# Trunk layer step on one core: the first channel products take turns with the modulation, and the last expert's rows are finished on chip

## The reference

```python
sh1, sc1, g1, sh2, sc2, g2 = jnp.split(mod, 6)         # mod = silu(c) @ w_mod + b_mod, w_mod is 1024 x 6144
u = rmsnorm(x, norm1_g) * (1 + sc1) + sh1
z = u @ w_in                                           # 1024 x 5120: xr, xv, xg, ga, gb
...                                                    # RG-LRU branch on xr, conformer branch on xv, xg
merged = sigmoid(ga) * (y_a @ w_rnn_out) + sigmoid(gb) * (y_b @ w_conv_out)
x = x + g1 * (merged @ w_out)
v = rmsnorm(x, norm2_g) * (1 + sc2) + sh2
x = x + g2 * ec_moe(v, w_router, w_e1, w_e3, w_e2)     # 16 experts, each takes its top 64 + 16 tokens
y = rmsnorm(x, final_norm_g)                           # for both token sets
```

## Time and profile before

| | |
|---|---|
| time, median of 3 runs | 1774.56 us (1773.85 to 1776.88) |
| the profiled execution | 1772.81 us, of it 1771.0 us span from first to last instruction |
| TensorE busy | 1655.0 us, 93% of the span |
| VectorE, ScalarE busy | 1401.4 us (79%), 1096.5 us (62%) |
| data moved | 492.49 MB, 278 GB/s over the span |

### The profile page before, as it was taken

How to read it: one execution, slowest core, us unless ns; L and a number is a source line. 1 busy time by engine, 2 the same in 40 slices (tenths; PEclk the granted TensorE clock), 3 DMA queues, 4 the chain that set the end, 5 groups by cost and what they waited for, 6 DMA issues and landing times.

```text
span 1771.0 us, 20907 instructions
## 1 busy us (share of the span) xinstructions
PE 1655.0 (93%) x7922; PEld 1168.0 (66%) x7922; DVE 1401.4 (79%) x1306; ACT 1096.5 (62%) x839; POOL 262.5 (15%) x124
## 2 busy tenths in 40 slices
PE   4698889899999949999999999999999999999994
PEld 0298779688888736666666666666666666666662
DVE  0429999997335468998998898898988989989985
ACT  3325544552522347777778777777777777777773
POOL 2002536420000010102201101102101012022020
PEclk8699999999999969999999999999999999999997
DMA  9811120122325289999999999999999999999993
GB/s 392 321 53 48 53 71 30 60 72 71 98 72 167 100 328 397 361 383 389 374 377 386 372 380 384 370 381 384 374 389 370 379 392 363 384 389 363 382 336 126
DMA packets 142559, 492.49 MB, mean 278 GB/s; under 512 B 11258, under 2 KB 23706, under 8 KB 139457
## 3 DMA queue, kind: packets, MB, share of 16 engines
q1 hardware_dynamic: 137280, 475.75, 71.3%
q0 software_dynamic: 3776, 11.09, 2.8%
q10 hardware_dynamic: 1472, 5.25, 0.7%
HBM read 478.91 MB, written 13.16 MB: 278 GB/s over the span
## 4 chain that ended last, share of the span: by engine, by line
PE 82%; DVE 10%; DMA 5%; issue 1%; ACT 1%; another core or an unknown queue 0%; SPq 0%; DVEq 0%; POOLq 0%; ACTq 0%
PE ps L1803 60%; PE ps L1618 12%; DVE ring L1116 5%; DMA ring<-in_w_mod 3%; PE ps L1580 2%; PE ps L1678 2%; PE ps L1730 1%; DVE ring L1144 1%; PE ps L1783 1%; DVE a_lo L1050 1%; PE ps L1515 1%; PE ps L1595 1%; DVE ring L1091 1%; DMA xn_dram<-ring 1%; PE ps L1777 0%
## 5 line engine op out<-in xcount | busy, mean ns | idle before, releaser
L1420 DVE TENSOR_TENSOR ring_lo<-ring,w_hi 128x2048 fp32r<-128x2048 f32 x384 | 872.2, 2289 | 109.5 <-ACT w_hi L918 109.5
L918 ACT ACTIVATE w_hi<-ring 128x2048 fp32r<-128x2048 f32 x384 | 734.9, 1918 | 260.1 <-PE ps L1803 259.9
L1803 PE MATMUL ps<-w_hi,xe_hi 128*80 128x512 f32 x1024 | 403.1, 394 | 2.1 <-DVE xe_lo L1481 2.1
L1803 PE MATMUL ps<-ring_lo,xe_hi 128*80 128x512 f32 x1024 | 402.8, 393 | 0.0
L1803 PE MATMUL ps<-w_hi,xe_lo 128*80 128x512 f32 x1024 | 400.6, 391 | 0.0
L1803 PEld LDWEIGHTS ps<-w_hi,xe_hi 128*80 128x80 f32 x1024 | 151.8, 148 | 86.5 <-issue 2.9
L1803 PEld LDWEIGHTS ps<-w_hi,xe_lo 128*80 128x80 f32 x1024 | 151.8, 148 | 84.3 <-issue 0.7
L1803 PEld LDWEIGHTS ps<-ring_lo,xe_hi 128*80 128x80 f32 x1024 | 151.8, 148 | 80.9 <-issue 0.5
L653 POOL DMA_INDIRECT acc_dram<-ya,idx_s x16 | 75.5, 4717 | 864.7 <-remote 864.7
L1803 PE MATMUL ps<-w_hi,h_hi 128*80 128x512 f32 x512 | 203.1, 397 | 0.0
L1803 PE MATMUL ps<-ring_lo,h_hi 128*80 128x512 f32 x512 | 201.1, 393 | 0.0
(11 more groups left out here) (266 smaller groups left out, 2008.8 us busy)
## 6 DMA issues: line engine op xcount, KB each, us to landing
ring<-in_w_e SPq DMA_DIRECT2D x192, 2048.0 KB, 9.7
ring<-in_w_mod SPq DMA_DIRECT2D x24, 1024.0 KB, 15.8
ring<-in_w_in SPq DMA_DIRECT2D x12, 1024.0 KB, 5.1
ring<-in_w_in SPq DMA_DIRECT2D x16, 512.0 KB, 3.7
xr<-in_x_sample SPq DMA_DIRECT2D x8, 512.0 KB, 5.5
ring<-in_w_rnn_out SPq DMA_DIRECT2D x8, 512.0 KB, 3.8
ring<-in_w_conv_out SPq DMA_DIRECT2D x8, 512.0 KB, 3.9
ring<-in_w_out SPq DMA_DIRECT2D x8, 512.0 KB, 4.2
```

Source lines behind the costliest of these rows:

```text
L918: eng.activation(w_hi[m % 2][:, 2 * half:2 * half + 2, :], chunk(m)[:, 2 * half:2 * half + 2, :], ACT.Copy).then_inc(unit_hi, 1)
L1420: eng.tensor_tensor(w_lo(m)[:, 2 * half:2 * half + 2, :], w, w_hi[m % 2][:, 2 * half:2 * half + 2, :].bitcast(F32), ALU.subtract)\
L1803: ins = eng.matmul(ps[0:CAP, bank + b, :], x[:, k0 + kk, :], w[:, kk, 512 * b:512 * b + 512], start=first and kk == 0 and n == 0, stop=las ...
```

## The change

Five parts belong together at the start, three at the end.

Start: (1) SP puts two `w_in` tiles after the eighth `w_mod` piece and the third after the sixteenth. (2) The tokens are transposed and copied unscaled out of PSUM while the first third of mod is still being loaded; the copy of the column vectors (`cols`) comes behind it on DVE, the reciprocal of the norm before it. (3) Scale and shift are applied in place in SBUF, and the split runs by pairs of 128-row blocks (four pairs) instead of halves. (4) The first round of the channel loop is taken out of the loop and its six groups stand between the second and third thirds of mod on TensorE; the gates begin the loop, and the other banks of `MOD_BANKS` and `MOD_TURN_BANKS` keep the two apart. (5) ACT and DVE are reordered to suit.

End: (6) the last expert stands outside the loop and leaves out the unused rows. (7) When the fifteenth addition has landed and two of the ring's slots are free, SP reads `acc_dram` back, and the five tiles are normed and stored without the last expert. (8) POOL gathers the last expert's 80 rows of `acc_dram`; its `ye` is added to them on DVE, squared, normed, and written by two indirect transfers over the stored rows.

The core of the diff:

```diff
-MOD_BANKS = (4, 5, 4)
+MOD_BANKS = (4, 6, 2)
+MOD_TURN_BANKS = (7, 7, 3)
...
+        fin = ring[:, 0:NT * D].rearrange("p (t d) -> p t d", t=NT)
...
@@ sync @@
-            for n in range(2 * KD):
+            for n in range(KD):
                 load_mod(n)
-            for kind in range(3):
-                load_a(0, kind)
+            load_a(0, 0)
+            load_a(0, 1)
+            for n in range(KD, 2 * KD):
+                load_mod(n)
+            load_a(0, 2)
...
-            eng.wait_ge(scattered, 16 * E)
+            product_done(eng, E - 1, NSLOT)
+            product_done(eng, E - 1, NSLOT + 1)
+            eng.wait_ge(scattered, 16 * (E - 1))
             for t in range(NT):
-                eng.dma_start(xr[:, t, :], acc_dram[P * t:P * t + P, :]).then_inc(fin_loaded[t], 16)
+                eng.dma_start(fin[:, t, :], acc_dram[P * t:P * t + P, :]).then_inc(fin_loaded, 16)
...
@@ gpsimd, after the loop of E - 1 @@
+            eng.indirect_dma_start(out=xe, out_offset=None, in_=acc_dram,
+                                   in_offset=bass.IndirectOffsetOnAxis(ap=idx_t[:, E - 1:E], axis=0)).then_inc(xe_loaded, 16)
...
+            eng.wait_ge(out_stored, 16 * NT)
+            eng.wait_ge(out_ready, NT + 1)
+            for out, column, lo, hi in ((a["y_sample"][0], 0, 0, CAP_S), (a["y_prompt"][0], 1, CAP_S, CAP)):
+                eng.indirect_dma_start(out=out, out_offset=bass.IndirectOffsetOnAxis(ap=idx_out[0:hi - lo, column:column + 1], axis=0),
+                                       in_=ye[lo:hi, :], in_offset=None).then_inc(rows_patched, 16)
@@ scalar @@
+            for k in range(KD):
+                eng.wait_ge(xt_turned, k + 1)
+                eng.activation(uT[:, k, 0:NP], ps[:, 2 * (k % 2) + 1, 0:NP], ACT.Copy).then_inc(xt_prompt, 1)
             copy_mod(0)
...
+                for k in (2 * j, 2 * j + 1):
+                    eng.activation(uT[:, k, 0:NP], uT[:, k, 0:NP], ACT.Identity, scale=a1[:, k, 0:1], bias=modc[:, k, 0:1])\
+                        .then_inc(ut_prompt, 1)
...
+                eng.activation(u_hi[:, 2 * j:2 * j + 2, :], uT[:, 2 * j:2 * j + 2, :], ACT.Copy).then_inc(u_hi_ready, 1)
@@ vector @@
+                    eng.tensor_scalar(uT[:, k, NP:N], uT[:, k, NP:N], a1[:, k, 1:2], modc[:, k, 1:2], ALU.mult, ALU.add)\
+                        .then_inc(ut_sample, 1)
...
+            output(E - 1)
+            eng.wait_ge(ye_ready, E)
+            eng.wait_ge(xe_loaded, 16 * (E + 1))
+            eng.tensor_tensor(ye, ye, xe, ALU.add).then_inc(ye_ready, 1)
...
+            eng.scalar_tensor_tensor(out=ye, in0=ye, scalar=rstat[0:CAP, 3, 0:1], in1=gf[0:CAP, :],
+                                     op0=ALU.mult, op1=ALU.mult).then_inc(out_ready, 1)
@@ tensor @@
+            channel_products(0, 0, first=True)
+            channel_products(0, 1)
+            eng.wait_ge(cols_ready, 1)
+            for n in range(KD, 2 * KD):
+                mod_products(n)
+            channel_products(0, 2)
+            mod_turn(1)
+            eng.wait_ge(modc_ready, 2)
+            channel_products(0, 3)
+            eng.wait_ge(xr_copied, 2)
+            for n in range(2 * KD, 3 * KD):
+                mod_products(n)
+            channel_products(0, 4)
+            mod_turn(2)
+            eng.wait_ge(modc_ready, 3)
+            channel_products(0, 5)
+            with eng.Fori(0, 3) as i:
+                gate_products(i)
+                for n in range(6):
+                    channel_products(i + 1, n)
+            gate_products(3)
```

More of the change, by code:

```diff
@@ L401, in trunk_layer @@
         gf_loaded = sem("gf_loaded")
-        fin_loaded = [sem(f"fin_loaded{t}") for t in range(NT)]
+        fin_loaded = sem("fin_loaded")
+        last_prompt_idx = sem("last_prompt_idx")
+        rows_patched = sem("rows_patched")
         fin_ssq = sem("fin_ssq")
@@ L645, in _ @@
             step.restart()
-            with eng.Fori(0, E) as i:
+            with eng.Fori(0, E - 1) as i:
                 eng.wait_ge(xe_turned, i + 2)
@@ L797, in _ @@
             a_high(0, 0, first=True)
-            a_high(0, 1, first=True)
+            eng.wait_ge(a12_ready, 1)
+            u_prompt(0)
+            u_prompt(1)
+            u_high(0)
+            u_prompt(2)
+            u_high(1)
+            u_prompt(3)
+            u_high(2)
+            u_high(3)
+            a_high(0, 1, first=True)
+            eng.wait_ge(cols_ready, 1)
+            lam = cols[:, C_TAB + 8 * G_LAM:C_TAB + 8 * G_LAM + 16]
+            step.did(eng.activation(sp[:, 0, :], lam, ACT.Abs))
+            step.wait()
+            eng.activation(sp[:, 1, :], sp[:, 0, :], ACT.Exp, scale=-1.0).then_inc(exp_lam_ready, 1)
+            step.restart()
+            a_high(0, 2, first=True)
+            eng.wait_ge(consts_ready, 4)
+            copy_xr(0)
+            copy_mod(1)
             copy_mod(2)
-            a_high(0, 2, first=True)
-            copy_xr(0)
+            eng.wait_ge(mod_used, 3 * KD)
             first_tap(0)
@@ L1002, in _ @@
             inverse_root(ssq_ready, NT, ms_ready, root_ready, 0, NT)
+            eng.wait_ge(root_ready, 1)
+            eng.reciprocal(rstat[:, 3, :], rstat[:, 2, :]).then_inc(r_ready, 1)
+            for k in range(KD):
+                eng.wait_ge(xt_turned, k + 1)
+                eng.tensor_copy(uT[:, k, NP:N], ps[:, 2 * (k % 2), :]).then_inc(xt_sample, 1)
             eng.wait_ge(cols_turned, 1)
             eng.tensor_copy(cols[:, 0:C_TAB + 8 * G_NLAM], ps[:, 6, 0:C_TAB + 8 * G_NLAM]).then_inc(cols_ready, 1)
-            eng.wait_ge(root_ready, 1)
@@ L1006, in _ @@
[L1006 removed]
+            eng.wait_ge(cols_ready, 1)
             mod_columns(0)
             modulated(a1, 1, C_N1)
[L1009 to L1016 removed]
+            eng.wait_ge(xt_sample, KD)
@@ L1458, in dve_expert @@
                         split_h(i, 1)
-                        modulate_xe(i + 2)
-                split_xe(i + 2)
+                        if not final:
+                            modulate_xe(i + 2)
                 if not final:
+                    split_xe(i + 2)
                     for m in range(2):
                         split_piece(i + 1, m)
-                output(i)
-                step.restart()
+                    output(i)
+                    step.restart()
+            eng.tensor_scalar(idx_out[:, 0:1], idx_t[0:CAP_S, E - 1:E], float(NP), None, ALU.subtract).then_inc(idx_ready, 1)
             split_piece(0, 0)
@@ L1538, in turn_row_tile, with turn_x @@
                 ins.then_inc(done, 1)
+            def turn_x(k):
+                turn_row_tile(xn1, k, 4, xt_turned, (xt_sample, xt_prompt))
             eng.wait_ge(silu_ready, 1)
-            for n in range(KD):
+            for n in range(5):
                 mod_products(n)
+            eng.wait_ge(xn1_ready, NT)
+            turn_x(0)
+            turn_x(1)
+            turn_x(2)
+            mod_products(5)
+            turn_x(3)
+            turn_x(4)
+            turn_x(5)
+            mod_products(6)
+            turn_x(6)
+            turn_x(7)
             eng.wait_ge(vec_loaded, 16 * 13)
@@ L1792, in _, with expert @@
                     ins.then_inc(xe_turned, 1)
-            with eng.Fori(0, E) as i:
+            def expert(i, final):
                 eng.wait_ge(xeT_ready, i * 2 + 1)
@@ L1829, in _ @@
                 eng.wait_ge(h1_silu, i * 2 + 2)
-                turn_xe(i + 2)
+                if not final:
+                    turn_xe(i + 2)
                 hidden_product(9)
@@ L1834, in _ @@
                 hidden_product(11)
+            with eng.Fori(0, E - 1) as i:
+                expert(i, False)
+            expert(E - 1, True)
 _INS = ["x_prompt", "x_sample", "state_rglru", "c", "c_ctx", "norm1_g", "norm2_g", "w_mod", "b_mod", "w_in",
```

146 lines of the change are left out of this document (71 added, 75 removed).

## The result

The changed kernel takes 1741.51 us (median of four runs, 1740.48 to 1741.78), the kernel before beside it 1774.20: a ratio of 0.9814 [0.9802, 0.9827], 32.7 us less. The forecast was 1743.5, 2.0 us too high. The profiled execution has a span of 1740.0 us, against 1771.0.

What follows compares the result with a forecast made beforehand. Two places bound it: the first round's 288 products, on which DVE's chain hangs, and 24 us behind the last product. 21 + 9 = 30 us off 1772.81 gave 1742.8; 1743.5 was called, range 1735 to 1757.

Steps and rivals of the forecast that it cites:

- Start: First round's six groups: done earlier, so DVE's chain starts 21 us sooner, carried to the end; bounds 10 and 25.
- Step 1: Normed rows ready near 23 us, token transposes between pieces 4 and 7; first third's columns at 42 us, before and after.
- Step 2: DVE's token scaling and splits: last quarter ready at 53.9 us; first product near 46.7, group 1 at 56.5, group 2 at 63.5.
- Step 3: Loads: piece 15 waits for piece 8's buffer, SP's queue stops, piece 15 lands at 69.5 us; products 8 to 15 end at 70.8.
- Step 4: Groups 3 and 4, last third's pieces: group 4 ends at 86.2 us, piece 23 lands at 92.8, with 2 us of waiting.
- rival (d): TensorE, interrupted by waits, stays at half clock up to group 6: costs 58 us, total 1800 us; chance 3%.
- Step 5: Group 6 ends at 108.9 us, before 130.5; DVE's chain starts 21.6 us earlier, taken as 21 and carried to the end.
- rival (e): DVE's first round waits for gate weights or next tiles; only the end gains: 1764 us, 3%; no end gain: 1773, 2%.
- Experts: Expert loop: body unchanged; last expert drops eight transposes, 0.55 us; the small scatter-index operation on DVE costs nothing.
- End: Behind the last product: final norm mostly done earlier, last transfer lands at 1761.7 against a span end of 1771.0; 9 us gained.
- the bound "3 us sooner": Last two indirect transfers: landing 3 us sooner than estimated would make the end's gain 12 us.
- the sign of 7 to 8 us: Kernel's end: the span was to end 7 to 8 us behind DVE's last scaling.

Runs made afterwards that it cites:

- the earlier tile: The changed kernel with the third `w_in` tile loaded ahead of `w_mod` piece 15 instead of behind it: 1737.07 us, 4.4 us less than the changed kernel.

## Why the prediction was right, point by point

**Start** (forecast 21 us, measured 22.7 at the split that opens DVE's stretch). The order of events is as forecast. That the number fits is in part luck, since two errors cancel in it.
- Step 1 is the worst: the columns of the first third stood at 37.0 and not at 42. I had kept TensorE's work "the same in another order" behind rows that end at 39.1; but the rows now start at 17.62, the transposes fall between pieces that were late anyway, and from 22 to 36 us the clock was full. That made 5 us.
- Step 2: the first product came at 41.78, 4.9 us ahead of 46.7, but at the lower clock to about 47. Groups 1 and 2 are done at 58.73 against the 63.5 forecast. At full clock a group took 7.2 to 7.3 us and not 7.0.
- Step 3 came true: the loads stood still from 54 to 60 us (DMA share 0.04 and less), and this cost TensorE nothing at piece 15, since products 8 to 15 ran in one go (7.08 us from 58.73).
- Step 4 names 2 us of waiting for piece 23, but its own sum holds only 0.2 (86.2 + 7 x 0.91 = 92.6, landing at 92.8). Measured were 2.35: TensorE came 5.1 us sooner (81.13 against 86.2), and the piece only 3.0 (89.8). The lower clock behind the wait (about 1.5 us) was rival (d) on a small scale, a few us and not 58. Three of the kernels above kept full clock behind waits of 2.20, 2.25 and 2.38 us, so the wait alone does not decide it. Group 6 ended at 107.8 against 108.9: of 5 us won by step 1 about 4 were lost again here, and the earlier tile shows that the wait can be had back.
- Step 5: DVE's chain hung on the sixth group and ACT's rounding, and the gain was carried on (21.6 us were left at the last expert): rival (e) falls.

No run takes the turns on TensorE and the earlier rows apart, so how much of the 22.7 us each of them made is not shown.

**Experts** (forecast 0.55). The 0.55 is there. "The one small operation for the scatter index ... nothing" failed: it moved POOL's first gather past the slot between two half splits, and the first expert's products came 2.2 us later for it. The Trainium skill has a rule of this kind ("SBUF — State Buffer", section "SBUF: two separate sides"): a DVE operation with two inputs in SBUF and a GpSimd operation that reads SBUF exclude one another for a whole instruction. The trace agrees in one direction: POOL's issue, which takes its row numbers from SBUF, ends 0.9 us behind the end of a half split in both kernels, and takes 1.01 us where it starts ahead of the split. In the other direction it shows no such block: there the split began 0.7 us before POOL was done, and took its usual 4.49 us. Why POOL misses the slot when it starts 0.20 us into the first half (5.17 us) and meets it when it starts 0.26 us into it (2.90) stays open.

**End** (forecast 9 us). The first square starts 1.4 us behind the end of the rounding (1717.2 and 1715.76; 1.5 forecast), and the output waited some 1.7 us for DVE (2.1 forecast). The two transfers were quicker than the row they were sized by: 0.93 and 0.86 us on POOL and 2.8 to 3.2 to landing, against 1.46 and 5.0. From POOL's start to the last landing it took 4.1 us where 6.5 were forecast, most of the bound "3 us sooner". The figure cited from the Trainium skill ("DMA: Bandwidth & Descriptors", section "Anatomy of one DMA — SWDGE (gpsimd) path") gave an estimate of 2.6 us for the larger one; here the trace, 3.2, lies nearer to it than to the 5.0 that I took.

That gain was lost to something that the prediction does not have: POOL's drain, 2.5 us behind the landing. The two errors cancel. That the 9 us came out right is therefore luck, and so is the sign of 7 to 8 us from DVE's last scaling to the end of the span (7.7). Reading back was hidden, as said. In all the end is worth 31.0 - 21.6 = 9.4 us in the spans, dropped transposes included, and 8.0 in the runs of the end alone with the slow gather in it.

## What to carry to other kernels

Here work interleaved to fill a wait moved the wait to the next transfer that stands behind a stopped queue: look for the last load that the queue's order delays, since one tile moved there was worth 4.4 us, some 2.4 of them the wait itself. An operation that costs nothing on its own engine can still shift what runs beside another engine's issue, so check what POOL's indirect transfers meet on DVE. If the last thing in a program is POOL's, count its drain.

## What was not expected of the hardware

- POOL's closing drain ends 4.3 to 4.5 us behind its last work, both behind an indirect transfer and behind a write of one element (0.09 us).
- POOL's issue of an 80-row gather took 1.01, 2.9 or 5.17 us, by where it fell among DVE's half splits of 2.25 us.
- An indirect transfer that only writes took 0.86 to 0.93 us on POOL and 2.8 to 3.2 us to landing; the accumulating one took 1.46 and 5.0 at best.
